# Retention on one core: rows centred by a matrix product, another order of a tile's steps, three query buffers, products moved to GpSimd

## The chip, the cores and the metric

The kernel runs on one core of a Trainium2 chip. The metric is the device time in microseconds of one launch, which computes the whole decoder step below. Its time is given as the median of the runs and their spread; a profile comes from one more execution, whose own time is given beside its span.

## What is computed

The reference is one inference step of a two-layer decoder, for a prompt of 2048 rows and 8 samples of 8 rows each. The even layer mixes attention and retention; the change touches retention and the gate that follows it. Cut to that:

```python
def retention_chunk(S0, q, k, v, log_gamma):          # chunks of 128 rows, S0 carried on
    scores = jnp.einsum('bihd,bjhd->bhij', q, k) * decay[None]
    o = jnp.einsum('bhij,bjhe->bihe', scores, v)
    o = o + jnp.einsum('bihd,bhde->bihe', q, S0) * q_dec[None, :, :, None]
    S1 = S0 * jnp.exp(L * log_gamma)[None, :, None, None] + jnp.einsum('bjhd,bjhe->bhde', k * k_dec[None, :, :, None], v)
    return o, S1

def even_out(fo, ro, g, gn_w, w_out):
    mu = jnp.mean(ro, axis=-1, keepdims=True)          # over the 64 entries of a head
    var = jnp.mean(jnp.square(ro - mu), axis=-1, keepdims=True)
    ro = ((ro - mu) * lax.rsqrt(var + NORM_EPS)).reshape(B, L, RET_W) * gn_w.astype(F32)
    cat = jnp.concatenate([fo.reshape(B, L, FOX_W), ro], axis=-1) * jax.nn.silu(g.astype(F32))
    return cat.astype(w_out.dtype) @ w_out
```

`fo` is what attention gave, `ro` retention's rows, `g` the gate. There are 8 heads of 64 entries, so rows of 512.

## The kernel before

The program runs its phases one after the other, with a barrier of all engines between them: input projection in two halves, forget gates, the samples' retention, attention, retention of the prompt, output projection, the recurrent layer in two halves, output projection. Each phase writes out what every engine does, in order; engines meet at semaphores. `Count.at(t)` names the value that a semaphore has when tile t's step is done.

`retention` (line 1630) works through 17 tiles of 128 rows: tiles 0 to 15 are the prompt, tile 16 holds the samples' rows, whose retention is there already (`ro`), so that they only need centring, scaling and gating. Six tiles matter in PSUM: `ps_q` (queries and keys turned), `ps_s` (scores), `ps_o` (retention's output, turned), `ps_u` (the state's update, and after it the output turned back, as `ps_r`), `ps_a` (the gated rows turned for the next phase).

For a prompt tile t the steps are these. TensorE: `turn_qk` (L1925, eight transposes), `score` (L1933, four products of 256 columns), `attend` (L1944 and L1948: for each pair of heads one product with the state, then two with the values), `add_to_state` (L1956, four products), `turn_rows` (L1964, four transposes of the output), `turn_gated` (L1971, eight transposes). ScalarE: `place` (L1785, L1788: keys and queries out of PSUM), `keep_o` (L1794), the square (L1804), the square root (L1808), `tanh_gate` (L1799), the rounded half of the gated rows, a_hi (L1815). VectorE: `decay_q` (L1836), `decay_scores` (L1841), `update` (L1847 decays the state, L1852 adds the update), `gate_silu` (L1858), `centre` (L1869, L1871, L1873: mean, scaling, centring; then L1876, the gate on attention's rows, called the fox product here), the sum of squares (L1882), var (L1884), the reciprocal (L1888), normed (L1890), gated (L1894), the rest of the rounding, a_lo (L1901). GpSimd: `decay_k` (L1765) and silu_gn (L1772, the SiLU times the norm's weights). SyncE issues the loads of q, k, v (two buffers), of gates and attention's rows (two buffers), and the stores of a_hi and a_lo.

The engines work a tile or two ahead of one another: in step t TensorE does attend for t+1, turns q and k of t+2, adds t+1 to the state, turns the rows of t+1 back, scores t+2 and turns the gated rows of t. `each_tile` makes these steps a loop of seven passes with two tiles in each, and writes the last three tiles out. Waits that the change touches: attend of t+1 waits until the scores are decayed, until the state holds tile t, and until `keep_o` of t is done; `turn_rows` waits for the copy of o and for the state's addition, since it writes over `ps_u`; the sum of squares waits for ScalarE's square, which waits for the centring.

In the input projection's second half (`in_proj`, L373 and L309) the two halves of the gate are copied from PSUM, one by VectorE, one by ScalarE.

## Time and profile before

| | us |
|---|---|
| median of 3 runs | 4133.45 |
| their spread | 4122.27 to 4133.8 |
| the profiled execution | 4131.24 |
| its span | 4129.6 |
| mean granted TensorE clock over the span | 0.924 |

The span reaches from the first to the last instruction. A granted clock of 1.0 is 2.4 GHz, 0.5 is 1.2 GHz; the mean of a stretch says how its time is shared between the two. Over the span TensorE is busy 3565.7 us (86%), VectorE 1694.8 us (41%), ScalarE 1380.3 us (33%) and GpSimd 371.6 us (9%). Retention is some 262 us of it, from the first load of its constants at 2304.45 to the last store's issue at 2564.42 with its landing. Shares over the whole span say little on such a stage; its own rows are read below.

### The profile page before, as it was taken

The numbers are of one execution on the slowest core, as the hardware profiler recorded it, in microseconds if no ns is written. First come the engines' busy times: TensorE is split into PE (matmuls) and PEld (weight loads), VectorE is DVE, ScalarE is ACT, GpSimd is POOL, SyncE is SP. The second block draws the span as 40 slices with busy tenths as digits, with TensorE's granted clock in tenths as the row PEclk, the third lists the DMA queues.
The fourth block names the chain that finished last, engine by engine and source line by source line (L and its number), as shares of the span: only waits on it lengthen the run. The fifth ranks groups of instructions, "written<-read, shape, count | busy, mean of one in ns | idle before, by whom it ended". The sixth has DMA issues, their size and how long they took to land. (4 is left out here: it accounts for less than half of the span.)

```text
span 4129.6 us, 65450 instructions
## 1 busy us (share of the span) xinstructions
PE 3565.7 (86%) x21028; PEld 2654.2 (64%) x21028; DVE 1694.8 (41%) x3182; ACT 1380.3 (33%) x2379; POOL 371.6 (9%) x630
## 2 busy tenths in 40 slices
PE   6999799946899899899999675899968949959998
PEld 5888688833455555555555453688856737748887
DVE  3222311143345445444444376433334645643333
ACT  3111200012233333333333254433335656642222
POOL 0000000010122222122223111000000000000000
PEclk9999899957799999999999786899988979979999
DMA  4233522255577777777775455433334233252221
GB/s 150 103 129 121 167 93 100 91 116 167 166 241 232 215 235 231 216 229 232 236 231 176 134 193 185 167 127 112 115 132 156 82 125 106 90 172 87 85 79 61
DMA packets 376166, 628.11 MB, mean 152 GB/s; under 512 B 125209, under 2 KB 175041, under 8 KB 375874
## 3 DMA queue, kind: packets, MB, share of 16 engines
q1 hardware_dynamic: 334098, 488.34, 36.3%
q0 software_dynamic: 41792, 136.48, 10.5%
q8 instruction: 126, 2.06, 0.2%
q14 instruction: 150, 1.23, 0.1%
HBM read 489.46 MB, written 135.22 MB: 151 GB/s over the span
## 5 line engine op out<-in xcount | busy, mean ns | idle before, releaser
L1549 PEld LDWEIGHTS att_samp_ps_t<-att_ident,att_samp_k_ring 128*128 128x128 f32 x2048 | 237.4, 146 | 281.5 <-issue 231.0
L1549 PE MATMUL att_samp_ps_t<-att_ident,att_samp_k_ring 128*128 128x128 f32 x2048 | 338.0, 290 | 84.5 <-DVE att_samp_kt L1354 44.6
L123 PE MATMUL in_ps_z<-in_w_hi,in_u_hi 128*128 128x512 f32 x952 | 375.7, 395 | 36.4 <-DVE in_w_lo L156 36.4
L124 PE MATMUL in_ps_z<-in_w_lo,in_u_hi 128*128 128x512 f32 x952 | 374.4, 393 | 0.0
L125 PE MATMUL in_ps_z<-in_w_hi,in_u_lo 128*128 128x512 f32 x952 | 374.3, 393 | 0.0
L1149 POOL DMA_DIRECT2D att_samp_v_ring<-cache_v x512 | 274.8, 537 | 984.5 <-issue 982.1
L1239 ACT COPY att_samp_kt<-att_samp_ps_t 128x512 f32<-128x512 f32 x256 | 149.8, 585 | 501.3 <-PE att_samp_ps_t L1549 500.6
L1354 DVE COPY att_samp_kt<-att_samp_ps_t 128x512 f32<-128x512 f32 x256 | 176.2, 688 | 292.4 <-PE att_samp_ps_t L1549 287.8
L1503 PE MATMUL att_fox_ps_o<-att_fox_prob,att_fox_v_one 128*65 128x512 f32 (+3 forms) x640 | 286.9, 532 | 3.8 <-ACT att_fox_prob L1208 3.8
L1303 DVE TENSOR_REDUCE att_fox_part_max<-att_fox_ps_n 128x1 f32<-128x512 f32 (+2 forms) x320 | 195.1, 610 | 131.1 <-PE att_fox_ps_n L1470 115.1
L1208 ACT ACTIVATE att_fox_prob<-att_fox_ps_k 128x512 f32<-128x512 f32 (+1 forms) x320 | 169.9, 536 | 189.5 <-DVE att_fox_ps_k L1322 110.5
L123 PEld LDWEIGHTS in_ps_z<-in_w_hi,in_u_hi 128*128 128x128 f32 x952 | 181.4, 190 | 75.8 <-issue 27.6
L123 PE MATMUL tail_ps_g<-tail_wg_hi,tail_h_hi 128*128 128x512 f32 x544 | 217.4, 400 | 11.0 <-DVE tail_p_lo L2196 9.9
L123 PE MATMUL tail_ps_o<-tail_wo_hi,tail_a_hi 128*128 128x512 f32 x544 | 214.3, 394 | 11.2 <-issue 8.7
L125 PE MATMUL tail_ps_g<-tail_wg_hi,tail_h_lo 128*128 128x512 f32 x544 | 213.6, 393 | 0.0
L124 PE MATMUL tail_ps_g<-tail_wg_lo,tail_h_hi 128*128 128x512 f32 x544 | 213.5, 392 | 0.0
L125 PE MATMUL tail_ps_o<-tail_wo_hi,tail_a_lo 128*128 128x512 f32 x544 | 213.4, 392 | 0.0
L124 PE MATMUL tail_ps_o<-tail_wo_lo,tail_a_hi 128*128 128x512 f32 x544 | 213.4, 392 | 0.0
L125 PEld LDWEIGHTS in_ps_z<-in_w_hi,in_u_lo 128*128 128x128 f32 x952 | 181.2, 190 | 38.2
L124 PEld LDWEIGHTS in_ps_z<-in_w_lo,in_u_hi 128*128 128x128 f32 x952 | 181.4, 191 | 37.4
L1588 PEld LDWEIGHTS att_samp_ps_v<-att_samp_v_ring,att_samp_prob_t 128*32 128x32 f32 x4096 | 118.5, 113 | 82.4 <-issue 71.2
L2224 DVE SCALAR_TENSOR_TENSOR tail_e<-tail_ps_g,tail_e 128x512 f32<-128x512 f32 x68 | 47.0, 692 | 278.6 <-ACT tail_ps_g L2162 278.6
(365 smaller groups left out, 6898.3 us busy)
## 6 DMA issues: line engine op xcount, KB each, us to landing
att_samp_v_ring<-cache_v POOLq DMA_DIRECT2D x512, 256.0 KB, 3.8
att_samp_k_ring<-cache_k SPq DMA_DIRECT2D x512, 256.0 KB, 3.5
tail_a_hi<-a_hi SPq DMA_DIRECT2D x34, 512.0 KB, 5.6
tail_a_lo<-a_lo SPq DMA_DIRECT2D x34, 512.0 KB, 5.9
in_w_stage<-w_in_even SPq DMA_DIRECT2D x64, 256.0 KB, 6.4
lru_u_hi<-u_hi SPq DMA_DIRECT2D x8, 2048.0 KB, 8.0
lru_u_lo<-u_lo SPq DMA_DIRECT2D x8, 2048.0 KB, 13.2
in_x<-x SPq DMA_DIRECT2D x17, 512.0 KB, 3.9
```

The source lines that it names most:

```text
L123: pe.matmul(out, act_hi, w_hi, start=start, stop=False)
L124: pe.matmul(out, act_hi, w_lo, start=False, stop=False)
L125: return pe.matmul(out, act_lo, w_hi, start=False, stop=stop)
L1149: pool.dma_start(v_ring[:, p, g, :], row(io["cache_v"], page)).then_inc(vp_in[y], 16)
L1208: act.activation(prob[:, s % 4, r:G], ps_k[:, s % 2, r:G], ACT.Exp).then_inc(exped.sem, 1)
L1239: act.copy(kt[:, n % 2, :, p * PAGE:(p + 1) * PAGE], ps_t[:, :].rearrange("p (a k) -> p a k", a=PAIRS)).then_inc(k_even.sem, 1)
L1303: dve.tensor_reduce(part_max[:, g, b % B4, c:c + 1], ps_n[:, 0:w], AX.X, ALU.max).then_inc(maxed.sem, 1)
L1354: dve.tensor_copy(kt[:, n % 2, :, p * PAGE:(p + 1) * PAGE], ps_t[:, :].rearrange("p (a k) -> p a k", a=PAIRS)).then_inc(k_odd.sem, 1)
L1503: pe.matmul(ps_o[0:HD + 1, r:G], v[:, par, kt, :], prob[:, s % 4, r:G], start=kt == 0, stop=kt == B4 * (g + 1) - 1).then_inc(weighed.sem, 1)
L1549: last = pe.transpose(ps_t[:, a * PAGE:(a + 1) * PAGE], k_ring[:, n % 2, p, a * P:(a + 1) * P], ident[:, :])
L1588: last = pe.matmul(ps_v[strip, g, :], prob_t[:, c % 2, at:at + 2 * R], v_ring[:, p, g, a * P:(a + 1) * P], start=c == 0 and p == 0, stop=c ...
L2224: dve.scalar_tensor_tensor(out=half(e, g), in0=ps_g[:, g, :], scalar=1.0, in1=half(e, g), op0=ALU.add, op1=ALU.mult)\
```

## The change

Arithmetic: the mean is taken off by TensorE. `turn_rows` no longer transposes the output with the identity but multiplies it with `centre`, a matrix of two blocks I - 1/64, so that the rows come back turned and centred in one product. They lie in `ps_o` in place of `ps_u`. VectorE's mean, scaling and centring remain for the samples' tile alone, once, ahead of the loop. The square on ScalarE and normed on VectorE read the centred rows from PSUM.

Work: the state's decay and the fox product go from VectorE to GpSimd. The factor 0.5 of the gate goes into the copies of the input projection.

Order and buffers: `attend` does its four products with the state first, then the eight with the values; it waits for normed of the tile before. The order of a step changes on all engines. Queries, keys and values get three buffers, the decayed queries and the gated rows two. The loop is written out for all 17 tiles.

```diff
+    c["centre"] = np.kron(np.eye(2), np.eye(HD) - 1.0 / HD)

-        ps_r = ps_u[:, :, :, :].rearrange("p a n e -> p (a n) e")
+        ps_r = ps_o[:, :, :].rearrange("p a (n e) -> p (a n) e", n=2)
...
+            def scale_state(t):
+                flat = state[:, :, :, :].rearrange("p a n e -> p (a n e)")
+                pool.wait_ge(*o_done.at(t))
+                pool.wait_ge(*added.at(t - 1))
+                pool.tensor_tensor(flat, flat, g_tab[:, :], ALU.mult).then_inc(scaled.sem, 1)
...
+                pool.wait_ge(gate_in[t % 2], 48 * (t // 2 + 1))
+                pool.wait_ge(*a_turned.at(t - 2))
+                pool.tensor_tensor(gated[:, t % 2, 0:W], fo[:, t % 2, :], silu[:, 0:W], ALU.mult).then_inc(fox_gated.sem, 1)
...
+            for t in range(-1, LAST):
+                if prompt(t + 1):
+                    decay_k(t + 1)
+                    scale_state(t + 1)
+                weigh_gates(t + 1)
...
             def step(t):
                 act.wait_ge(*var_made.at(t))
                 act.activation(var[:, 2, :], var[:, 1, :], ACT.Sqrt).then_inc(rooted.sem, 1)
                 if prompt(t + 2):
                     place(t + 2)
                 if t < LAST:
                     tanh_gate(t + 1)
+                if prompt(t + 1):
+                    keep_o(t + 1)
                 act.wait_ge(*a_turned.at(t))
                 act.wait_ge(a_stored, 32 * (t + 1))
                 act.copy(a_hi[:, :], ps_a[:, :]).then_inc(a_high.sem, 1)
+                if t < LAST:
+                    square(t + 1)
...
             def attend(t):
                 pe.wait_ge(*q_decayed.at(t))
                 pe.wait_ge(*sc_made.at(t))
                 pe.wait_ge(*added.at(t - 1))
-                pe.wait_ge(*o_kept.at(t - 1))
+                pe.wait_ge(*normed_rows.at(t - 1))
                 for a in range(PAIRS):
-                    pe.matmul(ps_o[:, a, :], state[:, a].rearrange("p n e -> p (n e)"), q_dec[:, a, :], start=True, stop=False,
+                    pe.matmul(ps_o[:, a, :], state[:, a].rearrange("p n e -> p (n e)"), q_dec[:, t % 2, a, :], start=a == 0, stop=False,
                               skip_group_check=True)
+                for a in range(PAIRS):
                     for half in range(2):
...
             def turn_rows(t):
                 pe.wait_ge(*o_kept.at(t))
-                pe.wait_ge(*added.at(t))
                 for a in range(PAIRS):
-                    last = pe.transpose(ps_u[:, a].rearrange("p n e -> p (n e)"), o_t[:, a, :], ident[:, :])
+                    last = pe.matmul(ps_o[:, a, :], o_t[:, a, :], centre[:, :], start=True, stop=True)
                 last.then_inc(r_turned.sem, 1)
...
-                    sp.wait_ge(*u_done.at(t + 1))
-                    fetch_qkv(t + 3, 1 - par)
+                    sp.wait_ge(*u_done.at(t))
+                    fetch_qkv(t + 3)
-                    sp.wait_ge(*gated_rows.at(t))
-                    fetch_gate(t + 2, par)
+                    sp.wait_ge(*fox_gated.at(t))
+                    fetch_gate(t + 2)
...
-                            dve.tensor_copy(z[:, g, :], ps_z[:, g, :]).then_inc(evac[g].sem, 1)
+                            dve.tensor_scalar(z[:, g, :], ps_z[:, g, :], 0.5, None, ALU.mult).then_inc(evac[g].sem, 1)
```

How the instructions stand on VectorE in a steady tile, before (from the second half of a loop's pass; `L1836` is the query product of tile t+2, `L1882` begins tile t+1):

```order
L1836 TENSOR_TENSOR ret_q_decayed<-ret_ps_q,ret_q_table 128x512
L1841 TENSOR_TENSOR ret_scores<-ret_ps_s,ret_decay 128x1024
L1901 TENSOR_TENSOR ret_a_lo<-ret_ps_a,ret_a_hi 128x1024
L1869 TENSOR_REDUCE ret_mean<-ret_ps_u 128x8
L1871 TENSOR_SCALAR ret_mean<-ret_mean 128x8
L1873 TENSOR_TENSOR ret_centred<-ret_ps_u,ret_mean 128x512
L1876 SCALAR_TENSOR_TENSOR ret_gated<-ret_fo,ret_silu 128x512
L1882 TENSOR_REDUCE ret_var<-ret_squares 128x8
L1884 TENSOR_SCALAR ret_var<-ret_var 128x8
L1847 TENSOR_TENSOR ret_state<-ret_state,ret_state_table 128x512
L1852 TENSOR_TENSOR ret_state<-ret_state,ret_ps_u 64x4x64 x2
L1888 RECIPROCAL ret_var<-ret_var 128x8
```

The same place after the change, from the query product of t+2 (`L1869` now) to the gated rows of t+1:

```order
L1869 TENSOR_TENSOR ret_q_decayed<-ret_ps_q,ret_q_table 128x512
L1890 SCALAR_TENSOR_TENSOR ret_silu<-ret_tanh,ret_gate 128x1024
L1882 TENSOR_TENSOR ret_state<-ret_state,ret_ps_u 64x4x64 x2
L1915 TENSOR_TENSOR ret_a_lo<-ret_ps_a,ret_a_hi 128x1024
L1875 TENSOR_TENSOR ret_scores<-ret_ps_s,ret_decay 128x1024
L1895 TENSOR_REDUCE ret_var<-ret_squares 128x8
L1897 TENSOR_SCALAR ret_var<-ret_var 128x8
L1899 RECIPROCAL ret_var<-ret_var 128x8
L1901 TENSOR_TENSOR ret_normed<-ret_ps_o,ret_var 128x512
L1906 TENSOR_TENSOR ret_gated<-ret_normed,ret_silu_gn 128x512
```

Four instructions between a_lo and the sum of squares and the state's decay are gone from VectorE; the state's addition has moved from behind var to ahead of a_lo, and the scores stand last before the sum.

TensorE before, in the second half of a loop's pass, from the last of the four pairs of attend (the first two rows, which stand four times) to the gated rows:

```order
L1944 MATMUL ret_ps_o<-ret_q_decayed,ret_state 128x128
L1948 MATMUL ret_ps_o<-ret_scores,ret_qkv 64x128 x2
L1925 MATMUL ret_ps_q<-ret_ident,ret_qkv 128x128 x8
L1956 MATMUL ret_ps_u<-ret_qkv,ret_k_decayed 128x128 x4
L1964 MATMUL ret_ps_u<-ret_ident,ret_o_turned 128x128 x4
L1929 REGISTER_ALU
L1933 MATMUL ret_ps_s<-ret_q_diagonal,ret_k_turned 128x256 x4
L1971 MATMUL ret_ps_a<-ret_ident,ret_gated 128x128 x8
```

TensorE after, one step (`L1940` turns q and k, `L1959` and `L1964` are attend, `L1988` turns the gated rows, `L1980` is turn_rows, `L1972` add_to_state, `L1948` the scores):

```order
L1940 MATMUL ret_ps_q<-ret_ident,ret_qkv 128x128 x8
L1959 MATMUL ret_ps_o<-ret_q_decayed,ret_state 128x128 x4
L1964 MATMUL ret_ps_o<-ret_scores,ret_qkv 64x128 x8
L1988 MATMUL ret_ps_a<-ret_ident,ret_gated 128x128 x8
L1980 MATMUL ret_ps_o<-ret_centre,ret_o_turned 128x128 x4
L1972 MATMUL ret_ps_u<-ret_qkv,ret_k_decayed 128x128 x4
L1948 MATMUL ret_ps_s<-ret_q_diagonal,ret_k_turned 128x256 x4
```

The gated rows of tile t have moved ahead of the next tile's turn_rows, q and k of t+2 are turned ahead of attend in place of behind it, and attend's two kinds of product no longer alternate. On GpSimd a step had two products and has four: k's decay, the state's decay, silu_gn and the fox product, in this order.

## Rows read from the trace of the kernel before

**Rows 1.** By stretch: length, busy us of PE, PEld, DVE, ACT, POOL, clock, DMA share, GB/s.
```profile
2340.63:2359.12 18.49, 15.53 (x85) 11.46 (x86) 10.14 (x17) 7.61 (x11) 2.53 (x2) 0.75 0.34 112
2359.12:2536.12 177.00, 132.24 (x784) 101.12 (x785) 132.40 (x208) 98.35 (x131) 33.42 (x26) 0.86 0.54 193
```

**Rows 2.** Timeline, VectorE and ScalarE, one tile: start, us, instruction, [idle before <-releaser].
```profile
2454.29 0.69 DVE L1882 TENSOR_REDUCE ret_var<-ret_squares 128x8 f32<-128x512 f32 x1 [0.18 <-ACT ret_squares L1804]
...
2455.01 0.17 DVE L1884 TENSOR_SCALAR ret_var<-ret_var 128x8 f32<-128x8 f32 x1
...
2456.04 0.21 ACT L1808 ACTIVATE ret_var<-ret_var 128x8 f32<-128x8 f32 x1
...
2456.09 0.85 DVE L1852 TENSOR_TENSOR ret_state<-ret_state,ret_ps_u 64x256 f32<-64x256 f32 x2 [0.30 <-PE ret_ps_u L1956]
...
2456.97 0.20 DVE L1888 RECIPROCAL ret_var<-ret_var 128x8 f32<-128x8 f32 x1
...
2457.21 0.69 DVE L1890 TENSOR_TENSOR ret_normed<-ret_centred,ret_var 128x512 f32<-128x512 f32 x1
...
2460.26 1.23 DVE L1858 SCALAR_TENSOR_TENSOR ret_silu<-ret_tanh,ret_gate 128x1024 f32<-128x1024 f32 x1 [1.63 <-ACT ret_tanh L1799]
...
2462.12 1.22 DVE L1841 TENSOR_TENSOR ret_scores<-ret_ps_s,ret_decay 128x1024 f32<-128x1024 f32 x1
2463.26 1.22 DVE L1901 TENSOR_TENSOR ret_a_lo<-ret_ps_a,ret_a_hi 128x1024 fp32r<-128x1024 f32 x1
...
2464.39 0.68 DVE L1869 TENSOR_REDUCE ret_mean<-ret_ps_u 128x8 f32<-128x512 f32 x1
...
2466.69 0.69 DVE L1882 TENSOR_REDUCE ret_var<-ret_squares 128x8 f32<-128x512 f32 x1
```

**Rows 3.** Timeline, TensorE, the same tile at the full clock.
```profile
2454.00 1.09 PE L1925 MATMUL ret_ps_q<-ret_ident,ret_qkv 128*128 128x128 f32 x8
...
2454.93 1.06 PE L1956 MATMUL ret_ps_u<-ret_qkv,ret_k_decayed 128*128 128x128 f32 x8
...
2457.09 0.63 PE L1964 MATMUL ret_ps_u<-ret_ident,ret_o_turned 128*128 128x128 f32 x4 [1.10 <-DVE ret_state L1852]
...
2463.44 0.46 PE L1944 MATMUL ret_ps_o<-ret_q_decayed,ret_state 128*128 128x128 f32 x2 [2.71 <-issue]
...
2463.83 0.44 PE L1948 MATMUL ret_ps_o<-ret_scores,ret_qkv 128*64 128x128 f32 x4
...
2466.56 0.66 PE L1925 MATMUL ret_ps_q<-ret_ident,ret_qkv 128*128 128x128 f32 x4
```

**Rows 4.** Timeline, TensorE, an earlier tile at the lower clock.
```profile
2421.89 0.77 PE L1944 MATMUL ret_ps_o<-ret_q_decayed,ret_state 128*128 128x128 f32 x2 [2.96 <-DVE ret_scores L1841]
2422.59 0.70 PE L1948 MATMUL ret_ps_o<-ret_scores,ret_qkv 128*64 128x128 f32 x4
...
2427.28 1.97 PE L1925 MATMUL ret_ps_q<-ret_ident,ret_qkv 128*128 128x128 f32 x8
2429.04 1.91 PE L1956 MATMUL ret_ps_u<-ret_qkv,ret_k_decayed 128*128 128x128 f32 x8
...
2432.94 3.06 PE L1933 MATMUL ret_ps_s<-ret_q_diagonal,ret_k_turned 128*128 128x256 f32 x8
```

**Rows 5.** Groups by line: busy us, mean ns, idle before, projection's copies on VectorE.
```profile
L373 DVE COPY in_z<-in_ps_z 128x512 f32<-128x512 f32 x17 | 11.8, 692 | 231.2 <-PE in_ps_z L125 231.2
```

**Rows 6.** Timeline, GpSimd and VectorE, the stage's first tile.
```profile
2333.84 1.27 POOL L1765 TENSOR_TENSOR ret_k_decayed<-ret_qkv,ret_k_table 128x512 f32<-128x512 f32 x1 [16.21 <-PE ret_ps_u L1956]
...
2334.75 1.44 DVE L1858 SCALAR_TENSOR_TENSOR ret_silu<-ret_tanh,ret_gate 128x1024 f32<-128x1024 f32 x1
...
2336.37 1.26 POOL L1772 TENSOR_TENSOR ret_silu_gn<-ret_silu,ret_gn_half 128x512 f32<-128x512 f32 x1 [1.26 <-DVE ret_silu L1858]
2336.94 0.71 DVE L1871 TENSOR_SCALAR ret_mean<-ret_mean 128x8 f32<-128x8 f32 x1
```

**Rows 7.** By tile, GpSimd's product of k: ns min/median/max, first and last start.
```profile
L1765 POOL TENSOR_TENSOR ret_k_decayed<-ret_qkv,ret_k_table x16: 1262/1265/1542, 2316.4 to 2524.5; 128x512 f32<-128x512 f32 x16
```

235 lines of the change are left out of this document (116 added, 119 removed).

## The prediction

> **What bounds the kernel now.** The change lies in the retention stage, 17 tiles (16 of the prompt, one of samples) between 2304 and 2569 us of the span. I read the busy time by stretch first, then the timeline of one tile on each engine, then the same tile's TensorE work at the lower clock. By stretch [rows 1], the 13 steps from the second tile's sum of squares to the fifteenth's take 177.00 us, 13.62 each; VectorE is busy 132.40 us, TensorE 132.24 us, ScalarE 98.35 us, GpSimd 33.42 us. No engine is full, so the step is a loop of waits. TensorE's mean granted clock is 0.86: (1 - 0.86) / 0.5 = 28% of the time at 1.2 GHz, the rest at 2.4.
>
> The timeline of a tile at the full clock [rows 2] shows the loop: it closes on VectorE, from one row sum of squares (2454.29) to the next (2466.69), 12.40 us. The VectorE rows follow one another, except for 1.63 us of idle before the SiLU (it waits for ScalarE's tanh). After the score product (2462.12) and a_lo (2463.26) come the mean, its scaling, the centring and ScalarE's square before the next sum: 2466.69 - 2464.39 = 2.30 us in which nothing else of the loop runs. TensorE [rows 3] sits idle 2.71 us before attend and then runs behind VectorE. When it falls to 1.2 GHz [rows 4], attend takes 2427.28 - 2421.89 = 5.39 us in place of 2466.56 - 2463.44 = 3.12, and the step lengthens: 13.62 - 12.40 = 1.2 us in the mean.
>
> **The change part by part.**
> *Off VectorE:* the mean, its scaling and the centring (the 2.30 us above, square included), the state's decay and the fox product, which go to GpSimd. In VectorE's loop this leaves: sum of squares, var, reciprocal, normed, gated, q, SiLU, state addition, a_lo, scores. VectorE alone no longer carries the step. The square now runs on ScalarE beside a_lo.
>
> *The new loop.* Attend must now wait for normed, since the centred rows lie in attend's own PSUM tile; and VectorE comes to the sum of squares only behind state addition, a_lo and scores. So the loop goes from normed through TensorE and back. At the full clock, step by step:
> - normed's end to attend: 0.10 (as from the scores' end, 2463.34, to 2463.44 [rows 2, 3]).
> - attend. The four state products come first, together. Eight such passes in a row go at 2454.93 - 2454.00 = 0.93; a state product of before takes 2463.83 - 2463.44 = 0.39 with its change of kind, so the eight value products have 3.12 - 4 x 0.39 = 1.56. Sum 2.49 [rows 3]. Bounds: 3.12 as before if the new order changes nothing; below 2.49 if the value products, too, run closer without the state products between them, by no more than these 1.56 would halve, 1.7. I take 2.49, since both paces are rows.
> - turn_gated, eight transposes: 0.93.
> - turn_rows: before, four transposes, x4 and 0.63 [rows 3]. Now four ordinary products with the centring matrix; add_to_state, also four products, stands as x8. So it takes 0.93 as well, and this is an addition to the path.
> - add_to_state to its end 1.06, then 0.04 to VectorE.
> - state addition 0.88 (2456.97 - 2456.09), a_lo 1.13, scores 1.13 (starts 2462.12, 2463.26, 2464.39), sum of squares 0.72, var 0.27 with the hop to ScalarE, square root 0.24, reciprocal 0.24, normed 0.69 [rows 2].
> Sum 10.84. One wait comes in: ScalarE copies o only behind the next tile's tanh, which ends 4.0 us after the square root (2456.25 to 2460.26 [rows 2]); the copy, 0.6 by an estimate from VectorE's 0.69 for the same width, ends at 4.6, and TensorE comes to turn_rows at 4.4. So 0.2 more: 11.0 us against 12.4.
>
> At 1.2 GHz [rows 4]: attend 1.76 + (5.39 - 4 x 0.70) = 4.35 (5.39 if the order brings nothing), turn_gated, turn_rows and add_to_state 1.76 each (2429.04 - 2427.28), and now the scores' products end later (3.06) than state addition and a_lo, so the path runs through them: 0.10 + 4.35 + 3 x 1.76 + 3.06 + 0.05 + 1.13 + 0.72 + 0.27 + 0.24 + 0.24 + 0.69 = 16.1 us.
>
> With 28% of the time at the lower clock the mean is 1 / (0.72 / 11.0 + 0.28 / 16.1) = 12.1 us. TensorE now lies on the path for about half the step, so a fall costs more than the 1.2 us of before; between 1.1 (this rule) and twice that I take 1.3, near the rule: 12.3 us. Saving 13.62 - 12.3 = 1.32, for 13 steps 17.2 us.
>
> *The first step* took 18.49 us at a clock of 0.75 [rows 1]; halfway between 11.0 and 16.1 it is 13.5: 5.0 us. *The start:* attend is 1.0 us shorter at the low clock, and the first square needs no mean, against a wider turn_rows and one more constant to load: 1.5 us by estimate, between 0 and 3. *The last step* loses mean, scaling, centring and square between a_lo and the sum, the 2.30 us of [rows 2], which stand there in the same order; the sample rows are centred at the start of the stage, when VectorE idles. The step before it has the TensorE path again: nothing taken.
>
> *At no cost:* the third query buffer moves SyncE's loads a tile earlier; no row of a steady tile shows TensorE waiting for qkv, so nothing is gained, and with the cover gone the price would be a transfer per tile. SyncE's gate loads wait for the fox product in place of the gated rows; behind this wait on its queue stand the a_hi and a_lo stores, which need a_lo, later in any case. The second buffers of q and gated take waits away that were not last. The unrolled loop saves at most 0.2 us in two tiles. The halving moved into the projection replaces 17 copies of 0.69 us by 17 products from PSUM of the same size, on a VectorE that idles 231.2 us before them [rows 5]: 0, at worst 17 x 0.5 us, hidden.
>
> *GpSimd* goes from two products to four a tile, 4 x 1.27 = 5.1 us of 11; behind the SiLU it runs three in a row. Does it reach the path? VectorE's small scaling, 0.17 us at 2455.01 [rows 2], took 0.71 from 2336.94, and ended with the GpSimd product that began at 2336.37 and took 1.26 [rows 6]: it was held until that product ended. In the new loop such a scaling (var) is on the path, 0.7 us behind the start of the sum of squares. Counted from that start, the square root ends at 1.2, tanh at 5.2, and attend, with it the release of the state's decay on GpSimd, at 4.8. A SiLU that met a GpSimd product (2334.75, the product from 2333.84 to 2335.11) took 1.44 in place of 1.23 [rows 2, 6], 0.2 more. By this row it ends at 6.7, the three products at 10.5, and var, at 11.7, is 1.2 us clear; the sum has nothing for GpSimd.
> The Trainium skill ("SBUF — State Buffer", section "Who interferes with whom") says that VectorE and GpSimd share a port pair as an exclusive lock, for VectorE's scalings and its products of two SBUF inputs alike, and that the second to come waits for the whole of the first. The row of the small scaling agrees; the SiLU's shows 0.2 where the product had 0.36 left. By the rule the SiLU would wait for the state's decay until 6.1 and end at 7.4, the products at 11.2: still 0.5 clear, and the sum the same 26 us, but one slow product would use it up (rival 2).
>
> **Sum.** 17.2 + 5.0 + 1.5 + 2.3 = 26.0 us. The profiled execution took 4131.24 us, 2.2 us under the median of 4133.45; from the median 4107.4 us, 0.63% faster.
>
> **The rivals.**
> 1. *The full clock holds.* For it: TensorE's work is contiguous from attend to the next turn_qk, with one pause a step. Against: by the sum that pause is some 2.8 us (11.0 less 2.49, 4 x 0.93, some 1.8 for the scores and the 0.2), between the 2.71 before an attend that kept the full clock and the 2.96 before one that did not [rows 3, 4]. Price: 13 x (13.62 - 11.0) + (18.5 - 11.0) + 1.5 + 2.3 = 45 us: 4088.
> 2. *GpSimd reaches the path.* The SiLU waits for the whole of the state's decay, to 4.8 + 1.27 = 6.1, ends at 7.4 and leaves the products 0.5 clear; and they take not 1.265 us, their median, but 1.542, their longest [rows 7]. Then var waits 4 x 0.28 - 0.5 = 0.6 us in each full-clock step: 0.72 x 13 x 0.6 = 5.6 us: 4113. For it speaks that 0.5 is less than the error on an 11 us sum; against it that most products took the median. The lock as the Trainium skill's page ("SBUF — State Buffer", the same section) states it would give the first half of this rival.
> 3. *Attend keeps its pace*: steps of 11.6 and 17.2, mean 12.9; 9 + 4 + 3.8 = 17 us: 4117.
> 4. *Half of the time at 1.2 GHz:* 13.1 a step; 7 + 3 + 3.8 = 14 us: 4119.
> 5. *Slower: the clock stays low.* TensorE's pause once a step brings a fall each time, and every step takes 16.1: 13 x (16.1 - 13.62) = 32 us lost, less 2.4 + 0.5 + 2.3: 4160. It decides from a mean step of 14.3 us, that is 73% of the time at the lower clock. Against it: at that clock TensorE would be busy 14.2 us of 16.1, its pause 1.9 us, shorter than any before a fall in these rows; and a mean of 0.86 says that the low stretches of before end.
> 6. *It does not do what it says:* that centring by a product leaves the loop where it was (a wait for something else last). Attend's wait for the state would be last only if the addition came after normed; it comes 4 us before. Small, and counted with 3.
>
> **How the numbers follow.** Forecast 0.43, rival 1 0.20, rival 2 0.13, 3 (with 6) 0.08, 4 0.10, 5 0.06. About 0.3%, 12 us, is what a measurement of this kernel can tell from no change. The forecast counts as faster with nine tenths (its own spread is some 8 us), rival 1 whole, 2 and 3 with three quarters, 4 with half: 0.39 + 0.20 + 0.10 + 0.06 + 0.05 = 0.80, taken as 0.78 since the order of waits is worked out and not seen; slower 0.06; the rest, 0.16, no change. The range reaches from rival 1's 4088 less a run's spread to rival 4's 4119 plus one: 4085 to 4124.
>
> **What would show it.** Right: steps of about 11 us at the full clock; attend near 2.5 us there; VectorE's sum of squares directly behind the scores; turn_rows as x8. Wrong: a pause on VectorE between sum and var that ends with a GpSimd product (rival 2); attend at 3.1 (3); a granted clock in the stage near 0.95 (1), 0.75 (4) or 0.55 (5). Were the clock at 0.86 and the steps still 13 us, the loop would be another than the one drawn here.

## The result, and the profile after

The changed kernel takes 4093.22 us in the median (4085.64 to 4099.52, 4 runs) against 4131.7 (4122.27 to 4133.8) of the kernel before, timed beside it: a ratio of 0.9911, 95% interval 0.9894 to 0.9929, that is 0.89% or 37 us faster. The forecast was 4107 with a range of 4085 to 4124. The profiled execution took 4094.79 us (4131.24 before), its span is 4093.0 (4129.6), the mean granted clock 0.928 (0.924).

By stretch, the first step and the thirteen steps cut as in [rows 1], with what lies ahead of them (from the first load of the constants) and behind (up to the next phase's first load). Columns: us; busy us and instructions of TensorE, its weight loads, VectorE, ScalarE, GpSimd; granted clock; DMA share; GB/s.

```profile
2307.14:2337.56 30.42, 13.49 (x80) 10.98 (x80) 8.48 (x13) 6.69 (x10) 6.39 (x5) 0.68 0.64 229
2337.56:2349.57 12.01, 9.12 (x64) 8.11 (x64) 7.46 (x13) 7.57 (x10) 5.46 (x4) 0.86 0.15 54
2349.57:2505.70 156.13, 117.42 (x824) 105.56 (x824) 101.55 (x144) 97.57 (x130) 67.78 (x52) 0.86 0.61 214
2505.70:2536.57 30.87, 10.22 (x64) 8.92 (x64) 14.10 (x23) 12.52 (x15) 6.26 (x5) 0.64 0.44 163
```

The thirteen steps take 156.13 us in place of 177.00, 12.01 each in place of 13.62, at the same granted clock of 0.86. VectorE's busy time falls from 132.40 to 101.55, GpSimd's doubles from 33.42 to 67.78. From the first load to the next phase's first load the stage takes 229.43 us in place of 265.04; the 35.6 us saved there are the gain of the span (36.6) but for 1 us.

VectorE in a steady tile (start us, us, engine, line, operation, names, shapes; behind it the idle time before and what ended it), and the SiLU of the tile after it:

```profile
2457.89 0.68 DVE L1895 TENSOR_REDUCE ret_var<-ret_squares 128x8 f32<-128x512 f32 x1
...
2463.02 1.23 DVE L1890 SCALAR_TENSOR_TENSOR ret_silu<-ret_tanh,ret_gate 128x1024 f32<-128x1024 f32 x1 [1.71 <-ACT ret_tanh L1815]
2466.58 0.85 DVE L1882 TENSOR_TENSOR ret_state<-ret_state,ret_ps_u 64x256 f32<-64x256 f32 x2 [2.34 <-PE ret_ps_u L1972]
2467.46 1.23 DVE L1915 TENSOR_TENSOR ret_a_lo<-ret_ps_a,ret_a_hi 128x1024 fp32r<-128x1024 f32 x1
2468.61 1.21 DVE L1875 TENSOR_TENSOR ret_scores<-ret_ps_s,ret_decay 128x1024 f32<-128x1024 f32 x1
2469.74 0.68 DVE L1895 TENSOR_REDUCE ret_var<-ret_squares 128x8 f32<-128x512 f32 x1
2470.45 0.17 DVE L1897 TENSOR_SCALAR ret_var<-ret_var 128x8 f32<-128x8 f32 x1
...
2474.86 2.31 DVE L1890 SCALAR_TENSOR_TENSOR ret_silu<-ret_tanh,ret_gate 128x1024 f32<-128x1024 f32 x1 [1.72 <-ACT ret_tanh L1815]
```

GpSimd, its last product of the first of these tiles and its first of the second:

```profile
2467.81 1.29 POOL L1770 TENSOR_TENSOR ret_k_decayed<-ret_qkv,ret_k_table 128x512 f32<-128x512 f32 x1
2474.82 1.27 POOL L1777 TENSOR_TENSOR ret_state<-ret_state,ret_state_table 128x512 f32<-128x512 f32 x1 [5.72 <-PE ret_ps_o L1964]
```

TensorE in both:

```profile
2460.12 2.04 PE L1959 MATMUL ret_ps_o<-ret_q_decayed,ret_state 128*128 128x128 f32 x8 [2.89 <-DVE ret_normed L1901]
2462.10 1.57 PE L1964 MATMUL ret_ps_o<-ret_scores,ret_qkv 128*64 128x128 f32 x16
2463.60 1.09 PE L1988 MATMUL ret_ps_a<-ret_ident,ret_gated 128*128 128x128 f32 x8
2464.53 1.06 PE L1980 MATMUL ret_ps_o<-ret_centre,ret_o_turned 128*128 128x128 f32 x8
2465.42 1.06 PE L1972 MATMUL ret_ps_u<-ret_qkv,ret_k_decayed 128*128 128x128 f32 x8
...
2471.97 1.13 PE L1959 MATMUL ret_ps_o<-ret_q_decayed,ret_state 128*128 128x128 f32 x8 [2.89 <-DVE ret_normed L1901]
...
2474.66 1.97 PE L1988 MATMUL ret_ps_a<-ret_ident,ret_gated 128*128 128x128 f32 x8
2476.43 1.22 PE L1980 MATMUL ret_ps_o<-ret_centre,ret_o_turned 128*128 128x128 f32 x8
```

This is the loop that the prediction drew: the sum of squares follows the scores without a gap; attend waits for normed; the state addition waits for add_to_state (2.34 us of idle VectorE); turn_rows stands as x8. TensorE idles 2.89 us ahead of each attend. Behind the pause its clock falls and recovers within the step, in these two tiles once in the state products (2.04 us in place of 1.13) and once in turn_gated (1.97 in place of 1.09); of the thirteen steps one, of 11.00 us, shows no fall, one takes 13.42 us, and the others lie between 11.84 and 12.07. In both tiles the stretch from attend's start to turn_rows takes 4.4 us (2460.12 to 2464.53; 2471.97 to 2476.43).

### The profile page after: what moved, and what is told of

Read it like the earlier page. It is cut to its first block and busy times, and to the rows that moved or that the text cites. A ratio compares the mean times of both kernels' runs of the same rounds, so it can differ in the third digit from the quotient of the medians.

```text
span 4093.0 us, 65190 instructions
## 1 busy us (share of the span) xinstructions
PE 3539.3 (86%) x21092; PEld 2654.0 (65%) x21092; DVE 1653.5 (40%) x3100; ACT 1379.3 (34%) x2379; POOL 415.3 (10%) x663
## 5 line engine op out<-in xcount | busy, mean ns | idle before, releaser
L1487 PE MATMUL att_fox_ps_k<-att_fox_q_a,att_fox_k_a 128*128 128x512 f32 (+1 forms) x320 | 160.2, 501 | 0.0
```

The source lines that it names most:

```text
L1487: pe.matmul(ps_k[:, s % 2, r:G], k_a[:, par, k], q_a[:, par, q], start=True, stop=False)
```

## The experiments

before_busy is an edit of the kernel before, all others start from the changed kernel: the next six lines of the table have one edit each, pairs_busy and vector_products_busy add that of busy16 to another, and the last three build on one another. Ratios are to the kernel before, run beside each; its medians there were 4128.75 to 4132.12, so differences between medians of this table can be off by some 3 us. The step is the mean of the same thirteen steps of the profile.

| run | median us | ratio, 95% interval | step us | granted clock in the steps |
|---|---|---|---|---|
| the changed kernel | 4093.22 | 0.9911 (0.9894 to 0.9929) | 12.01 | 0.86 |
| pairs | 4144.26 | 1.0028 (1.0013 to 1.0043) | 14.69 | 0.75 |
| vector_products | 4101.87 | 0.9929 (0.9917 to 0.9942) | 12.24 | 0.85 |
| centre_vector | 4133.63 | 1.0010 (0.9999 to 1.0021) | 14.42 | 0.79 |
| rows_transposed | 4084.62 | 0.9887 (0.9870 to 0.9904) | 11.09 | 0.92 |
| two_buffers | 4123.59 | 0.9975 (0.9965 to 0.9985) | 13.51 | 0.87 |
| busy16 | 4082.42 | 0.9886 (0.9871 to 0.9901) | 11.01 | 1.00 |
| before_busy | 4118.60 | 0.9967 (0.9958 to 0.9976) | 12.54 | 1.00 |
| pairs_busy | 4098.23 | 0.9920 (0.9907 to 0.9934) | 11.61 | 0.99 |
| vector_products_busy | 4096.87 | 0.9925 (0.9912 to 0.9939) | 11.97 | 1.00 |
| sum_first | 4075.73 | 0.9855 (0.9836 to 0.9874) | 10.38 | 0.95 |
| sum_first_act | 4050.18 | 0.9808 (0.9790 to 0.9827) | 9.38 | 1.00 |
| tanh_first | 4052.62 | 0.9817 (0.9804 to 0.9830) | 9.07 | 1.00 |

### The clock: busy16 and before_busy

```diff
+            def fill(t):
+                pe.wait_ge(*a_low.at(t - 1))
+                for k in range(16):
+                    pe.transpose(ps_a[:, k % KC * P:(k % KC + 1) * P], qkv[:, (t + 1) % QB, 0, 0:P], ident[:, :])
...
                 if prompt(t + 1):
+                    fill(t)
                     attend(t + 1)
```

Expected of busy16:

> The changed kernel with 16 extra transposes a tile put into TensorE's pause of 2.89 us ahead of attend (they go to ps_a, which turn_gated overwrites). In the changed kernel the granted clock falls once in every step behind that pause. Theory A (the pause brings the fall): with 16 transposes, 1.86 us at the full clock, the pause shrinks to some 1 us, the granted clock of the stage rises from 0.86 towards 1.0 and the step falls from 12.0 to about 11.0: 11 to 15 us faster than the changed kernel, 4078 to 4082. Theory B (the clock falls whether TensorE pauses there or not): the granted clock stays near 0.86, the time stays at 4093 or, where the extra work runs at the lower clock (3.5 us for a pause of 2.9), goes up by 0.6 us a step, to some 4102.

The thirteen steps, in the columns of the stretches above:

```profile
2344.81:2487.95 143.14, 123.98 (x1035) 110.79 (x1034) 102.07 (x144) 96.97 (x130) 65.44 (x52) 1.00 0.66 234
```

One of them on TensorE:

```profile
2402.09 1.13 PE L1959 MATMUL ret_ps_o<-ret_q_decayed,ret_state 128*128 128x128 f32 x8 [1.14 <-DVE ret_normed L1901]
2403.15 1.09 PE L1964 MATMUL ret_ps_o<-ret_scores,ret_qkv 128*64 128x128 f32 x16
2404.18 1.09 PE L1988 MATMUL ret_ps_a<-ret_ident,ret_gated 128*128 128x128 f32 x8
2405.56 1.16 PE L1980 MATMUL ret_ps_o<-ret_centre,ret_o_turned 128*128 128x128 f32 x8 [0.29 <-ACT ret_o_turned L1810]
```

And ScalarE beside it, tanh and the copy of o:

```profile
2403.84 1.06 ACT L1815 ACTIVATE ret_tanh<-ret_gate 128x1024 f32<-128x1024 f32 x1
2404.92 0.58 ACT L1810 COPY ret_o_turned<-ret_ps_o 128x512 f32<-128x512 f32 x1
```

Theory A: 1.9 us of extra work a tile on the engine that carries the path, and the kernel gets 11 us faster. With the pause down from 2.89 to 1.14 us the clock stays at 2.4 GHz and the steps last 11.00 to 11.02 us. This is also the full-clock step that the prediction had worked out as 11.0, with the wait of turn_rows for the copy of o behind tanh. (Ahead of tanh stands an ACT_TABLE_LOAD of 1.28 us on ScalarE in every step, ahead of the square root another; no run takes them away.)

For before the extra transposes go into ps_o and wait for the copy of o (keep_o).

```diff
+            def fill(t):
+                pe.wait_ge(*o_kept.at(t))
+                for k in range(16):
+                    pe.transpose(ps_o[:, k % PAIRS, :], ident[:, :], ident[:, :])
...
                 if prompt(t + 1):
+                    fill(t)
                     attend(t + 1, 1 - par)
```

> The kernel before with 16 extra transposes in its pause of 2.7 us ahead of attend (into ps_o, which attend overwrites). Theory A (at the full clock its loop is VectorE's, 12.40 us): the granted clock comes near 1.0 and steps are 12.4 to 12.6 us in place of 13.6; 13 x 1.1 and some 3 us of the first step: about 4114 us, and the change is then worth 1.4 us a step at an equal clock. Theory B (the low clock of before comes from another pause, or costs nothing there): the steps stay at 13.6, 4131 us or above.

The thirteen steps:

```profile
2365.13:2528.13 163.00, 134.16 (x989) 108.11 (x989) 131.67 (x208) 98.33 (x131) 33.10 (x26) 1.00 0.60 209
```

Theory A again: 12.54 us a step at clock 1.00; the median is 4118.60 where 4114 was expected. So the kernel before has a full-clock loop of 12.5 us and loses 1.1 us a step to the clock; the changed one has 11.0 and loses 1.0. At an equal clock the change is worth 1.53 us a step, nearly all of the 1.61 that it brought.

### The order of attend's products: pairs and pairs_busy

```diff
                 for a in range(PAIRS):
-                    pe.matmul(ps_o[:, a, :], state[:, a].rearrange("p n e -> p (n e)"), q_dec[:, t % 2, a, :], start=a == 0, stop=False,
+                    pe.matmul(ps_o[:, a, :], state[:, a].rearrange("p n e -> p (n e)"), q_dec[:, t % 2, a, :], start=True, stop=False,
                               skip_group_check=True)
-                for a in range(PAIRS):
                     for half in range(2):
```

> The changed kernel with attend's products in the order of before (a pair's state product, then its two value products). Theory A (attend lies on the path, and the grouped order is what shortened it): attend goes from 2.09 us at the full clock (first tile of the changed kernel) to 3.12, and the step grows by 0.6 to 1.0 us; 16 steps make 10 to 16 us: about 4103 to 4109 us, ratio to before 0.993 to 0.996. Theory B (the order of the products brings nothing): 4093 us, ratio 0.991.

The thirteen steps:

```profile
2348.22:2539.15 190.93, 152.50 (x824) 120.08 (x824) 95.78 (x144) 97.88 (x130) 65.68 (x52) 0.75 0.50 175
```

TensorE from one attend's start to turn_rows:

```profile
2421.26 0.77 PE L1959 MATMUL ret_ps_o<-ret_q_decayed,ret_state 128*128 128x128 f32 x2 [2.89 <-DVE ret_normed L1901]
...
2426.64 1.97 PE L1987 MATMUL ret_ps_a<-ret_ident,ret_gated 128*128 128x128 f32 x8
2428.41 1.92 PE L1979 MATMUL ret_ps_o<-ret_centre,ret_o_turned 128*128 128x128 f32 x8
```

Both theories missed: not 0 and not 0.6 to 1.0, but 2.7 us a step, and the kernel is no longer faster than before: 0.28% slower by the medians, and 9 us longer in the profile from the first load to the last sum of squares (260.22 against 251.24). In the tile shown attend alone takes 5.38 us (2421.26 to 2426.64), and the lower clock holds on through turn_gated and turn_rows; over the steps the granted clock is 0.75. One of the thirteen shows no fall: it lasts 11.49 us, with 3.13 us for attend (2350.44 to 2353.57). To price the order apart from the clock, both edits go together:

> Attend's products in the order of before, together with the 16 extra transposes in TensorE's pause, so that the order is priced with the clock held. Beside the changed kernel with the extra transposes alone (11.01 us a step, granted clock 1.00). Theory A (the order has a price of its own, and the lower clock multiplied it): attend goes from 2.15 to 3.12 us at the full clock; of this 0.4 us is absorbed, since turn_rows waits for ScalarE's copy of o behind tanh anyway; steps of 11.6 us, some 4091 us. Theory B (the order costs only through the clock): 11.0 us a step, 4082. If the granted clock does not come near 1.0 here, the extra transposes do not hold it in this order, and the price at the full clock stays open.

```profile
2363.41:2514.33 150.92, 135.53 (x1035) 113.54 (x1034) 95.81 (x145) 96.99 (x130) 73.11 (x52) 0.99 0.63 222
```

At the full clock the steps last 11.49 us (one, in which the clock fell, 13.01): theory A for the step. The median, 4098.23, is 7 us above its 4091: up to the last sum of squares the stage takes 10.8 us more than in busy16 (212.25 against 201.42), and the rest of the 16 us between the medians was not traced. The order itself costs 0.48 us a step; the other 2.2 of the 2.7 come through the clock. What of the order makes the lower stretch longer no run here shows.

### Centring: centre_vector and rows_transposed

```diff
+            def centre_rows(t):
...
+                dve.tensor_reduce(mean[:, 0, :], rows, AX.X, ALU.add).then_inc(sum_made.sem, 1)
...
+                dve.tensor_scalar(mean[:, 1, :], mean[:, 0, :], 1.0 / HD, None, ALU.mult).then_inc(mean_made.sem, 1)
...
+                dve.tensor_tensor(cen[:, :, :], rows, mean[:, 1, :].unsqueeze(2).broadcast_to([P, H, HD]), ALU.subtract)\
+                    .then_inc(centred.sem, 1)
...
                 if prompt(t + 2):
                     decay_scores(t + 2)
+                if t < LAST:
+                    centre_rows(t + 1)
...
-                pe.wait_ge(*normed_rows.at(t - 1))
+                pe.wait_ge(*centred.at(t - 1))
...
-                    last = pe.matmul(ps_o[:, a, :], o_t[:, a, :], centre[:, :], start=True, stop=True)
+                    last = pe.transpose(ps_o[:, a, :], o_t[:, a, :], ident[:, :])
```

> The changed kernel with the centring back on VectorE (row sums, scaling and subtraction behind the scores; turn_rows by four transposes; attend waits for the subtraction in place of normed). Theory A: VectorE then carries the loop: from the end of the subtraction to the square 0.7, sum and var 0.9, square root to tanh's end 4.1, SiLU 1.2 to 2.3, state addition 0.9, a_lo 1.1, scores 1.1, centring 1.65: 11.7 to 12.8 us a step against the 12.0 of the changed kernel, so 0 to 14 us slower than it, 4093 to 4107. Theory B (the centring by TensorE is the whole gain): back to the step of before, 13.6, about 4125 to 4131 us.

VectorE, the gated product and the state addition of one tile, and the stretch from the scores' end to the sum of squares of the next:

```profile
2440.54 1.80 DVE L1906 TENSOR_TENSOR ret_gated<-ret_normed,ret_silu_gn 128x512 f32<-128x512 f32 x1
...
2446.43 0.85 DVE L1882 TENSOR_TENSOR ret_state<-ret_state,ret_ps_u 64x256 f32<-64x256 f32 x2 [1.67 <-PE ret_ps_u L1974]
...
2449.59 0.68 DVE L1859 TENSOR_REDUCE ret_mean<-ret_ps_o 128x8 f32<-128x512 f32 x1
...
2451.90 0.69 DVE L1895 TENSOR_REDUCE ret_var<-ret_squares 128x8 f32<-128x512 f32 x1 [0.70 <-ACT ret_squares L1820]
```

Theory B in the time: without the centring by TensorE nothing is left of the gain. The stretch from the scores' end to the sum of squares is back whole, 2451.90 - 2449.59 = 2.31 us (2.30 in [rows 2]), and the step grows by 2.41; what of this is the lower clock, 0.79 in place of 0.86, was not priced. Theory A failed at a wait that I had left out: the state addition still waits for add_to_state, and TensorE reaches that only behind turn_gated, which waits for gated. The loop through TensorE stays, with the centring in it. In four of the thirteen steps gated, whose inputs both lie in SBUF, also meets GpSimd's product of the state's decay and takes 1.63 to 1.80 us in place of 0.69 (in the tile shown the product begins at 2440.53 and takes 1.26).

What the wider turn_rows costs, the change's one addition to the path:

```diff
-                    last = pe.matmul(ps_o[:, a, :], o_t[:, a, :], centre[:, :], start=True, stop=True)
+                    last = pe.transpose(ps_o[:, a, :], o_t[:, a, :], ident[:, :])
```

> The changed kernel with turn_rows as four transposes in place of four products with the centring matrix (the rows are then not centred at all: this part of the computation is left out). Theory A (turn_rows lies on the path, and a product stands as two passes where a transpose stands as one): 0.4 us shorter at the full clock, 0.8 at the lower: 0.4 to 0.7 us a step, 6 to 11 us faster than the changed kernel, 4082 to 4087. Theory B (turn_rows is covered, for instance by ScalarE's a_hi): 4093.

Theory A in size: 8.6 us between the medians, and of the steps (10.51 to 11.61 us) those at the full clock are 0.5 us shorter than 11.0. The rest of the 0.92 us a step comes with the clock, 0.92 in place of 0.86.

### Query buffers: two_buffers

```diff
-        QB = 3
+        QB = 2
...
-                    sp.wait_ge(*u_done.at(t))
+                    sp.wait_ge(*u_done.at(t + 1))
                     fetch_qkv(t + 3)
```

> The changed kernel with two query buffers in place of three (the loads of tile t+3 wait for add_to_state of t+1). Theory A: the loads are hidden either way: within 3 us of 4093. Theory B (the third buffer is needed): TensorE waits for qkv ahead of turn_qk, up to 1 us a step, 4100 to 4109.

TensorE:

```profile
2403.70 1.06 PE L1973 MATMUL ret_ps_u<-ret_qkv,ret_k_decayed 128*128 128x128 f32 x8
2404.59 1.89 PE L1949 MATMUL ret_ps_s<-ret_q_diagonal,ret_k_turned 128*128 128x256 f32 x8
2409.83 1.09 PE L1941 MATMUL ret_ps_q<-ret_ident,ret_qkv 128*128 128x128 f32 x8 [3.35 <-DMA ret_qkv<-rv]
```

The first load's issue on SyncE's queue:

```profile
2404.79 0.34 SPq L1731 DMA_DIRECT2D ret_qkv<-rq  x1
```

This wait over the thirteen steps (us in total, times, longest):

```profile
PE ret_ps_q L1941 <- DMA ret_qkv<-rv: 45.9, 13, 4.4
```

Theory B, and more than its 1 us: 1.5 us a step. From the first load to the last sum of squares this makes 21 us in the profile; between the medians 30 us, most of the change's gain. TensorE waits 3.5 us a step here (45.9 / 13); the step grows by less, since this wait takes the place of the 2.89 us ahead of attend, which are gone (0.2 us in all thirteen steps). The loads start when add_to_state ends (2404.79) and are there at 2409.8, 5.0 us later. In the changed order only the four score products stand between add_to_state and turn_qk; before, turn_rows, score, turn_gated and the next attend did. The buffer was not needed there and is needed here.

### Products on GpSimd: vector_products and vector_products_busy

```diff
             def add_update(t):
...
+                dve.wait_ge(*o_done.at(t))
...
+                dve.tensor_tensor(flat, flat, g_tab[:, :], ALU.mult).then_inc(scaled.sem, 1)
                 dve.wait_ge(*scaled.at(t))
...
             def gate_silu(t):
...
+                dve.tensor_tensor(gated[:, t % 2, 0:W], fo[:, t % 2, :], silu[:, 0:W], ALU.mult).then_inc(fox_gated.sem, 1)
```

> The changed kernel with the state's decay and the fox product back on VectorE, the decay directly ahead of the state addition, the fox product behind the SiLU. Theory A (the loop closes through TensorE, VectorE idles 1.5 to 2.3 us ahead of the state addition): 0.6 + 0.7 = 1.3 us of added work fit into that idle time, the SiLU is no longer held by a GpSimd product (1.23 us in place of 2.31), and the time stays within 3 us of 4093, ratio 0.991. Theory B (the relief of VectorE is what made the kernel faster): 1.3 us a step come back, some 20 us, about 4113 us, ratio 0.9955.

The medians are 8.7 us apart and the intervals of the ratios overlap; the medians fit neither theory, A with 3 us at most or B with 20. The steps differ by 0.23 us, 3 us in thirteen, and the start, up to the first sum of squares, by 2.4 (32.80 against 30.42; attend of tile 0 ran at the lower clock there). So in the steps theory A holds, but not for its reason, as the next run shows. With the clock held:

> The state's decay and the fox product back on VectorE, together with the 16 extra transposes. Theory A (these two products fit into VectorE's idle time ahead of the state addition): 11.0 us a step as with the extra transposes alone, 4082 us within 3. Theory B (at the full clock that idle time, 1.0 us behind a SiLU of 1.71 us, is too short for 1.3 us of products): 11.1 to 11.4 us a step, 4084 to 4089.

VectorE, the state's decay and its addition:

```profile
2418.76 1.76 DVE L1870 TENSOR_TENSOR ret_state<-ret_state,ret_state_table 128x512 f32<-128x512 f32 x1
2420.55 0.85 DVE L1875 TENSOR_TENSOR ret_state<-ret_state,ret_ps_u 64x256 f32<-64x256 f32 x2
```

GpSimd beside it:

```profile
2418.19 1.78 POOL L1775 TENSOR_TENSOR ret_silu_gn<-ret_silu,ret_gn 128x512 f32<-128x512 f32 x1 [8.49 <-DVE ret_silu L1883]
```

Theory B, with a larger price than it gave: 11.97 us a step at clock 1.00 against 11.01. The decay on VectorE starts 0.57 us into GpSimd's remaining product and ends 0.55 us after it (2420.52 against 2419.97), 1.76 us in place of 0.69. The update was there at 2419.51 (add_to_state 2418.45 + 1.06). So the split is worth 1.0 us a step at the full clock. In vector_products the decay takes 1.76 us as well; there, at the mixed clock, the longer TensorE path covers all but 0.2 of it.

### A shorter loop: sum_first, sum_first_act, tanh_first

The loop runs through state addition, a_lo and scores one behind the other, but a_lo has its inputs before the state addition has, and the sum of squares needs none of the three.

```diff
                 dve.tensor_scalar(var[:, 1, :], var[:, 0, :], 1.0 / HD, EPS, ALU.mult, ALU.add).then_inc(var_made.sem, 1)
+                if prompt(t):
+                    add_update(t)
+                if prompt(t + 1):
+                    decay_scores(t + 1)
                 dve.wait_ge(*rooted.at(t))
...
                 if t < LAST:
                     gate_silu(t + 1)
-                if prompt(t + 1):
-                    add_update(t + 1)
                 dve.wait_ge(*a_high.at(t))
                 dve.tensor_tensor(a_lo[:, :], ps_a[:, :], a_hi[:, :].bitcast(F32), ALU.subtract).then_inc(a_low.sem, 1)
-                if prompt(t + 2):
-                    decay_scores(t + 2)
```

> The changed kernel with another order on VectorE: a_lo directly behind the SiLU, then sum of squares, var, state addition, scores, reciprocal, normed. Theory A (the loop closes through a_lo, state addition and scores one behind the other): a_lo starts when a_hi is there, 1.7 us sooner, the square root lies beside the state addition, and the step gets 1.1 us shorter: 17 us, about 4076. Theory B (something else sets the step, as TensorE's own work at the lower clock): no change, 4093. Apart from both: var's small scaling now lies beside GpSimd's products; if it is held by them as the SiLU is (2.31 us in place of 1.23), it takes 0.5 to 1.3 us in place of 0.17 and eats the gain.

One passage on VectorE:

```profile
2416.65 0.68 DVE L1895 TENSOR_REDUCE ret_var<-ret_squares 128x8 f32<-128x512 f32 x1
2417.36 1.15 DVE L1897 TENSOR_SCALAR ret_var<-ret_var 128x8 f32<-128x8 f32 x1
```

The GpSimd product beside it:

```profile
2417.22 1.26 POOL L1770 TENSOR_TENSOR ret_k_decayed<-ret_qkv,ret_k_table 128x512 f32<-128x512 f32 x1
```

All seventeen vars (duration in ns: least, median, most; first and last start):

```profile
L1897 DVE TENSOR_SCALAR ret_var<-ret_var x17: 171/872/1166, 2343.8 to 2507.6; 128x8 f32<-128x8 f32 x17
```

Theory A (17.5 us between the medians), and the effect told apart from both comes too: var, eight numbers a row, begins 0.14 us into a GpSimd product and ends 0.03 us after it. In the changed kernel all seventeen take 0.17 us. So var's scaling goes into the square root:

```diff
-                act.activation(var[:, 2, :], var[:, 1, :], ACT.Sqrt).then_inc(rooted.sem, 1)
+                act.activation(var[:, 2, :], var[:, 0, :], ACT.Sqrt, scale=1.0 / HD, bias=eps[:, 0:1]).then_inc(rooted.sem, 1)
...
-                dve.tensor_scalar(var[:, 1, :], var[:, 0, :], 1.0 / HD, EPS, ALU.mult, ALU.add).then_inc(var_made.sem, 1)
```

> As the order with the sum of squares first, and var's scaling is taken into ScalarE's square root, so that nothing between the sum of squares and the reciprocal can be held by a GpSimd product. If GpSimd's products hold var in the other kernel: 0.5 to 1.3 us a step faster than that one; if not, 0.1 to 0.2 us a step (one small instruction less). By theory A (loop through a_lo, addition and scores): 4074 us or less, and TensorE's pause shrinks by 1.1 us to 1.8; if that lets the clock stay up, another 10 us. By theory B (TensorE at the lower clock sets the step): 4093.

The thirteen steps:

```profile
2344.09:2465.99 121.90, 101.81 (x833) 88.95 (x832) 98.96 (x131) 99.77 (x131) 65.14 (x53) 1.00 0.78 274
```

TensorE's pause:

```profile
2413.45 1.13 PE L1956 MATMUL ret_ps_o<-ret_q_decayed,ret_state 128*128 128x128 f32 x8 [1.37 <-DVE ret_normed L1904]
```

Steps of 9.37 to 9.38 us, 1.0 less than with var on VectorE (part of it is the clock, 0.95 there and 1.00 here); TensorE's pause is 1.37 us, and the clock stays at 2.4 GHz without any extra work. The kernel takes 4050.18 us, 1.9% less than before and 1.1% less than the changed kernel: it beats both.

```diff
                 act.activation(var[:, 2, :], var[:, 0, :], ACT.Sqrt, scale=1.0 / HD, bias=eps[:, 0:1]).then_inc(rooted.sem, 1)
+                if t < LAST:
+                    tanh_gate(t + 1)
                 if prompt(t + 2):
                     place(t + 2)
-                if t < LAST:
-                    tanh_gate(t + 1)
...
+                if t < LAST:
+                    gate_silu(t + 1)
                 if prompt(t + 2):
                     decay_q(t + 2)
-                if t < LAST:
-                    gate_silu(t + 1)
```

> As the kernel with the sum of squares first and var's scaling in the square root, and with tanh ahead of the copies of q and k on ScalarE, the SiLU ahead of the q product on VectorE. In that kernel the step is 9.38 us; ScalarE idles 1.28 us ahead of the copies, the SiLU waits 1.60 us for tanh and is then held by a GpSimd product (1.82 us), and a_lo comes behind it. Theory A (the loop closes through tanh and the SiLU): the SiLU ends before attend's end, a_lo waits for a_hi alone, and the score products become the last: attend 2.1, turn_gated, turn_rows, add_to_state 0.9 each, score products 1.9, their product with the decay 1.1, reciprocal 0.25, normed 0.7, hops: 8.8 to 9.0 us a step, 4041 to 4044 us. Theory B (something else closes it): 9.4, 4050.

All its SiLUs on VectorE (ns: least, median, most):

```profile
L1891 DVE SCALAR_TENSOR_TENSOR ret_silu<-ret_tanh,ret_gate x17: 1218/1218/1225, 2332.6 to 2477.7; 128x1024 f32<-128x1024 f32 x17
```

The steps shrink to 9.07 us, the SiLU is nowhere held, and a_lo waits for a_hi alone, as theory A has it; what closes the loop is then a_hi and a_lo, not the score products. The 4 us that this makes in thirteen steps do not show in the time: the intervals of the two kernels overlap for the larger part. Whether it is worth anything is open.

## Why the prediction was right

Right in sign, in the loop and in the range; 14 us too high. Of these, 10 lie between the profiled executions (36.5 us apart, 26.0 forecast) and 4 between these and the medians. Rival 1's 4088 lies nearer to the 4093 measured, though its mechanism was not there. The terms against the profile of the changed kernel:

| term | predicted saving | measured |
|---|---|---|
| start, to the first sum of squares | 1.5 | 36.18 - 30.42 = 5.8 |
| first step | 5.0 | 18.49 - 12.01 = 6.5 |
| thirteen steps | 17.2 | 177.00 - 156.13 = 20.9 |
| the step before the last | 0 | 9.85 - 10.71 = -0.9 |
| last step | 2.3 | 9.72 - 7.07 = 2.7 |
| behind the last sum | 0 | 13.80 - 13.09 = 0.7 |
| sum | 26.0 | 35.6 |

*The full-clock loop, 11.0:* 11.00 in the one full-clock step of the changed kernel, 11.01 throughout with the clock held. It holds by two errors that nearly cancel. Attend takes 2.09 us (2402.09 to 2404.18), not 2.49: the value products run closer, too, once the state products no longer stand between them, 1.03 us in place of the 1.56 that I carried over from [rows 3]; the bound of 1.7 had allowed for it. Because attend ends sooner, turn_rows waits longer for the copy of o behind tanh: 1.38 us pass between the starts of turn_gated and turn_rows, 0.45 more than turn_gated's 0.93, where I had 0.2. The other terms together are 0.1 off. The pause ahead of attend is 2.89 us, where rival 1 worked out some 2.8.

*The low clock:* the mean granted clock stayed at 0.86, as assumed; that was taken over from before and not worked out, and came true by luck: in the changed kernel's edits it lies between 0.75 and 1.00. But the step came to 12.01, not 12.3. No step ran at 1.2 GHz throughout, as the mixture of 11.0 and 16.1 has it: the clock falls behind the pause in all but one of the thirteen steps and takes 1.0 us between attend and turn_rows in the tiles shown (4.4 us against 2405.56 - 2402.09 = 3.47). This is 0.3 x 13 = 3.8 us of the miss, with rounding the whole of the third row.

*Start and first step:* 5.8 us of the miss, the largest share; both terms were sized too small. A little of it is the luck of one execution: in the profile of the changed kernel attend of tile 0 ran at 2.4 GHz, in that of before at 1.2, after the same work at the same distance from the stage's start (the last section). But in two_buffers, where it ran at 1.2 too, the two stretches take 32.17 + 11.15 = 43.32 us, against 42.43 here, 54.67 before and 48.2 by the forecast, so this clock accounts for some 0.9 us at most. Which part of the start saved more than the 1.5 us no run shows.

*What was put at no cost:* the third query buffer did bring nothing over before, and the price with the cover gone, a transfer a tile, was named. But it stands under "at no cost" for the wrong reason: I looked for a TensorE wait in the rows of before, where turn_qk stands behind attend. In the new order it stands right behind the score products, and without the buffer most of the gain is gone (30 of 37 us between the medians, 21 of 36 in the stage). The loop written out was priced at 0.2 us in two tiles at most, and before_busy's steps fit that: most alternate between 12.45 and 12.62 us. The halving, the second buffers of q and gated and the gate loads were not undone alone.

*Off VectorE:* the 2.30 us between scores and sum of squares were the right place and the right size (2.31 when put back). That GpSimd's share of the relief is worth little was not said; it is 0.2 us a step here, and 1.0 once the clock is held.

*The rivals.* 1, the full clock holds: its time was near, its mechanism was not there (granted clock 0.86, not 0.95); with the pause filled it comes about, at 4082 (4088 by its sum). 2, GpSimd reaches the path: not here. In six of the thirteen steps the SiLU does wait for the state's decay, in the others it takes 1.23 us. In the tile shown it takes 2.31 us from 2474.86, when GpSimd's product had begun at 2474.82 and took 1.27: 1.08 us of wait where 1.23 were left. That is the wait for the whole product that the Trainium skill ("SBUF — State Buffer", section "Who interferes with whom") states, and not the 0.2 us that my sum had from the row of before. I had misread that row: 0.21 us of wait where 0.36 were left, and 0.54 where 0.69 were left for the small scaling [rows 6], fall short of the product's end by the same 0.15 us. But in the tile shown GpSimd's last product of the step ends at 2469.10, and var begins at 2470.45. With var moved ahead of scores the rival is there at once (0.87 us in the median). 3, attend keeps its pace: excluded by attend's 2.09 us. 4, half of the time at 1.2 GHz: granted clock 0.86. 5, slower since the clock stays low: not in this kernel, and only in part one edit away. With attend in the old order (rivals 3 and 4 in one) the clock is 0.75 and not 0.55, the step 14.69 and the kernel 0.28% slower than before. I had argued that a pause at the low clock would be short, 1.9 us; in pairs it is 2.89 as in the changed kernel, since the clock has recovered when the score products run. 6: the centring does what it says.

*The parts do not add.* Undone one at a time, the order of attend costs 2.7 us a step, the centring 2.4, the buffer 1.5, the split 0.2: 6.8 us together, where the whole change brought 1.6. Each part presupposes others: rows centred in attend's own PSUM tile put TensorE into the loop, where attend's order counts (it was not tried alone in the kernel before), and turn_qk's new place needs the third buffer.

## What to carry to other kernels

When a change moves the loop from one engine to another, cost each part in the new loop: a buffer or an order of products that was worth nothing in the old one can be worth most of the gain. Where TensorE pauses once a step, look at what stands right behind the pause: the lower clock falls on it, and closing the pause, with idle work or better by a shorter loop on the engine that it waits for, was worth 1 us a step here. A small VectorE instruction on the path has no price of its own when GpSimd runs products back to back (var took 0.17 us or up to 1.17, by what it met); take it to ScalarE or keep it clear of them.

## What was not expected of the hardware

The same attend ran at either clock in kernels whose TensorE had done the same work up to it; of each kernel one execution was profiled. In the changed kernel and in two_buffers attend of tile 0 begins 20.93 and 20.70 us after the stage's first load, behind the same work and the same pause of 1.4 us. In the changed kernel:

```profile
2328.07 1.13 PE L1959 MATMUL ret_ps_o<-ret_q_decayed,ret_state 128*128 128x128 f32 x8 [1.37 <-issue]
2329.13 1.09 PE L1964 MATMUL ret_ps_o<-ret_scores,ret_qkv 128*64 128x128 f32 x16
```

In two_buffers:

```profile
2328.65 2.05 PE L1960 MATMUL ret_ps_o<-ret_q_decayed,ret_state 128*128 128x128 f32 x8 [1.36 <-issue]
2330.62 1.98 PE L1965 MATMUL ret_ps_o<-ret_scores,ret_qkv 128*64 128x128 f32 x16
```

In the kernel before, 20.92 us after its first load, it began at the lower clock too (0.77 us for the first product, 0.46 at the full clock in [rows 3]):

```profile
2325.37 0.77 PE L1944 MATMUL ret_ps_o<-ret_q_decayed,ret_state 128*128 128x128 f32 x2 [1.36 <-issue]
```

In the changed kernel attend takes 2.1 us, in two_buffers 3.9, and the first sum of squares comes 30.42 and 32.17 us after that load. When the clock rises is thus not fixed by TensorE's work since the stage's start alone, and a term read from one execution's start carries an error of up to 1.8 us.
